# Placing the high and low weight blocks of one gated product at unequal 64-byte shifts

## The reference

```python
def swiglu(x, w_gate, w_up, w_down):
    return (jax.nn.silu(x @ w_gate) * (x @ w_up)) @ w_down

meta = jnp.broadcast_to(meta_tokens[None].astype(x.dtype), (B, N_META, D_MODEL))
h = jnp.concatenate([meta, x], axis=1)                       # 272 rows
h = h + 0.5 * swiglu(rmsnorm_2(h, ffn1_norm), ffn1_w_gate, ffn1_w_up, ffn1_w_down)
```

## Time and profile before

| | |
|---|---|
| median of 3 runs | 912.51 us |
| the runs | 918.71, 912.08, 912.51 us |
| the profiled execution's own time | 918.25 us |
| its span | 916.5 us |
| PE, PEld | 904.2 us (99%), 887.5 us (97%) |
| DVE, ACT | 642.7 us (70%), 525.4 us (57%) |
| granted clock of TensorE, mean | 0.997 |
| sw1 in the span | 355.66 to 486.86 us |

### The profile page before, as it was taken

How to read it: one execution, slowest core, us unless ns; L and a number is a source line. 1 busy time by engine, 2 the same in 40 slices (tenths; PEclk the granted TensorE clock), 3 DMA queues, 4 the chain that set the end, 5 groups by cost and what they waited for, 6 DMA issues and landing times.

```text
span 916.5 us, 18478 instructions
## 1 busy us (share of the span) xinstructions
PE 904.2 (99%) x7425; PEld 887.5 (97%) x7425; DVE 642.7 (70%) x1108; ACT 525.4 (57%) x869; POOL 4.7 (1%) x11
## 2 busy tenths in 40 slices
PE   9999999999999999999999999999999999999996
PEld 8988998999999999999999999999999999999996
DVE  6999888776446765676666547768769877767553
ACT  6897877666336655544444535445675665454452
POOL 1000000000000000000000000000000000000000
PEclk9999999999999999999999999999999999999998
DMA  9751444365765565555556465554415655665641
GB/s 312 248 171 72 139 139 161 93 206 187 234 185 179 175 192 183 171 176 171 179 185 202 149 184 161 161 171 130 162 50 203 186 185 187 198 201 198 208 138 46
DMA packets 110612, 157.63 MB, mean 172 GB/s; under 512 B 9916, under 2 KB 61248, under 8 KB 110400
## 3 DMA queue, kind: packets, MB, share of 16 engines
q1 hardware_dynamic: 109776, 155.19, 53.4%
q10 hardware_dynamic: 576, 0.73, 0.2%
q0 software_dynamic: 176, 0.53, 0.1%
HBM read 155.37 MB, written 1.05 MB: 171 GB/s over the span
## 4 chain that ended last, share of the span: by engine, by line
PE 95%; DVE 3%; ACT 1%; issue 1%; DVEq 0%; ACTq 0%
PE ps L1046 29%; PE ps L1048 29%; PE ps L1047 29%; PE ps L1093 1%; PE ps L1129 1%; PE ps L1060 1%; DVE wl L1819 1%; PE ps L1303 0%; PE ps L1323 0%; PE ps L1261 0%; PE ps L1283 0%; PE ps L1139 0%; ACT wh L1385 0%; DVE S L2070 0%; PE ps L1152 0%
## 5 line engine op out<-in xcount | busy, mean ns | idle before, releaser
L1819 DVE TENSOR_TENSOR wl<-raw,wh 128x1024 fp32r<-128x1024 f32 (+2 forms) x291 | 346.8, 1212 | 197.4 <-ACT wh L1385 196.8
L1385 ACT ACTIVATE wh<-raw 128x1024 fp32r<-128x1024 f32 (+2 forms) x291 | 298.1, 1046 | 193.4 <-PE ps L1048 193.0
L1046 PE MATMUL ps<-U,wh 128*128 128x256 f32 (+2 forms) x1392 | 398.3, 286 | 0.1
L1048 PE MATMUL ps<-U,wl 128*128 128x256 f32 (+2 forms) x1392 | 391.4, 281 | 0.0
L1047 PE MATMUL ps<-UL,wh 128*128 128x256 f32 (+2 forms) x1392 | 390.8, 281 | 0.0
L1046 PEld LDWEIGHTS ps<-U,wh 128*128 128x128 f32 (+1 forms) x1392 | 261.6, 188 | 3.1 <-issue 1.4
L1047 PEld LDWEIGHTS ps<-UL,wh 128*128 128x128 f32 (+1 forms) x1392 | 261.9, 188 | 1.7 <-issue 1.0
L1048 PEld LDWEIGHTS ps<-U,wl 128*128 128x128 f32 (+1 forms) x1392 | 262.3, 188 | 0.0
L1046 PE MATMUL ps<-H,wh 128*128 128x256 f32 (+1 forms) x736 | 208.7, 284 | 0.1
L1048 PE MATMUL ps<-H,wl 128*128 128x256 f32 (+1 forms) x736 | 206.6, 281 | 0.0
L1047 PE MATMUL ps<-HLO,wh 128*128 128x256 f32 (+1 forms) x736 | 206.4, 280 | 0.0
(11 more groups left out here) (340 smaller groups left out, 788.5 us busy)
## 6 DMA issues: line engine op xcount, KB each, us to landing
raw<-w_ff SPq DMA_DIRECT2D x64, 512.0 KB, 4.4
raw<-ffn_w_gate SPq DMA_DIRECT2D x88, 256.0 KB, 3.7
raw<-ffn_w_up SPq DMA_DIRECT2D x88, 256.0 KB, 4.6
raw<-ffn_w_down SPq DMA_DIRECT2D x44, 512.0 KB, 4.6
raw<-w_in SPq DMA_DIRECT2D x40, 512.0 KB, 3.7
raw<-w_out SPq DMA_DIRECT2D x16, 512.0 KB, 3.9
raw<-wkv_x SPq DMA_DIRECT2D x8, 512.0 KB, 3.9
raw<-w_in SPq DMA_DIRECT2D x9, 256.0 KB, 3.1
```

What stands on the lines that cost most here:

```text
L1046: e.matmul(out, sh, xh, start=(i == 0 and n == 0), stop=False)
L1048: mm = e.matmul(out, sl, xh, start=False, stop=(over and n == nk - 1))
L1385: e.activation(wh, raw, ACT.Copy).then_inc(*up("w_hi", v))
L1819: lo = e.tensor_tensor(wl, raw, wh.bitcast(F32), ALU.subtract)
```

## The change

`first_columns` gets one more argument, 0 for the high blocks and 1 for the low ones. For sw1 alone it adds a number of columns from a table of eleven pairs, one pair per group. A column is 4 bytes, so 16, 32 and 48 are 64, 128 and 192 bytes. `tile` and `unit_parts` pass the argument, so PE, ACT and DVE agree on the places. All else is as it was.

```diff
+APART = ((0, 32), (32, 0), (0, 16), (16, 0), (0, 48), (48, 0), (16, 48), (48, 16), (32, 48), (16, 32), (32, 16))
+
+
-def first_columns(name, g, i):
+def first_columns(name, g, i, low):
...
-    return at
+    return [c + APART[g][low] for c in at] if name == "sw1" else at
...
-def split_blocks(parts, half, name, g, i):
-    at, width = first_columns(name, g, i), GEMM[name].width(g)
+def split_blocks(parts, half, name, g, i, low=0):
+    at, width = first_columns(name, g, i, low), GEMM[name].width(g)
...
-        wh, wl = split_blocks(t["wh"], h, name, g, i), split_blocks(t["wl"], low_half(h), name, g, i)
+        wh, wl = split_blocks(t["wh"], h, name, g, i), split_blocks(t["wl"], low_half(h), name, g, i, 1)
...
-    return raw, split_blocks(t["wh"], half, name, g, i), split_blocks(t["wl"], low_half(half), name, g, i)
+    return raw, split_blocks(t["wh"], half, name, g, i), split_blocks(t["wl"], low_half(half), name, g, i, 1)
```

## The result

| | before | after |
|---|---|---|
| median of 16 runs each | 912.1 us | 917.54 us |
| ratio, 95% interval | | 1.0047 [1.0027, 1.0066] |
| the shorter kind | 12 runs, 911.70 to 912.51 | 8 runs, 913.56 to 914.60 |
| the longer kind | 4 runs, 918.53 to 918.80 | 7 runs, 920.47 to 921.08 |
| the profiled execution, its span | 918.25, 916.5 us | 920.47, 918.6 us |

One execution of 4483 us stands outside both kinds; nothing here explains it. With eight executions in the shorter kind and eight above it, the median of 16 is the mean of 914.60 and 920.47 and falls between the kinds; the median of the other 15 would be 914.60. Within a kind the change costs 1.9 us (medians 911.98 and 913.90) and 2.1 us (918.71 and 920.76). The rest of the 5.4 us between the medians comes from the mixture alone. In both kinds the change makes less than 1% of difference.

What follows compares the result with a forecast made beforehand. PE's matmul steps were taken to bound the kernel. Adding 2.0 us for sw1's groups 1 to 10 and 0.1 us for group 0 to a short run's 912.51 us gave 914.6 us, range 911.2 to 921.3.

Steps and rivals of the forecast that it cites:

- The bound: Whole kernel: PE busy 904.2 of 916.5 us, so its length is the number of matmuls times the step between starts.
- The size: sw1: groups 1 to 10 go from 123.7 to 125.8 ns a step; with group 0, +2.1 us in all.
- the steps of uq, gq and small over their floor: 256-column products at other distances: 118.3 and 120 ns against 113.3, giving 125.0 and 126.7 at 272 columns; middle 125.8.
- The splits at nothing, dn1 unchanged: DVE and ACT splits in sw1 cost nothing more (1053 and 1224 ns); dn1 only starts 2.1 us later.
- Distance between load and stream: sw1, groups 1 to 10: weights load 64 bytes ahead of the stream in all three matmuls; other distances lengthen the step.
- Two changes of distance in three loads: Every changed sw1 group: 1 to 3 of three loads leave distance 64, and the distance changes twice in three loads.
- groups 0, 2 and 4: sw1 groups with unshifted high blocks: expected nearer 11.9 us than groups 5 to 10, most groups at 11.9 to 12.3.
- The median: Whole kernel: a short run's 912.51 us plus 2.1 gives 914.6 us as the median; chance 0.43.
- the chance of the longer kind: Whole kernel: the median falls among long executions, at 920.4 us (919 to 923), by the same mechanism; chance 0.25.
- (b): sw1: addresses do nothing, every group stays at 11.87 us, total 912.5 us; chance 0.12.
- (c): sw1: faster, since some shifts reach the 120.0 ns floor (group of 11.52 us); total 908.6 to 912 us; chance 0.15.
- (d): sw1: every load pays 10 ns, 133.7 ns a step, +10.6 us, total 923.1 us; chance 0.05.

Runs made afterwards that it cites:

- e6: Changed kernel plus one unit of ff1a (group 1, unit 0) shifted by 192 bytes; ten executions at 919.93 to 921.04 us, one far outside (1997.95).
- e5: Kernel before the change, with one unit of ff1a (group 1, unit 0) shifted by 192 bytes; eleven executions at 918.00 to 918.78 us.
- e1: Changed kernel, but sw1's groups take equal high and low shifts (0 to 192 bytes) and sw2 the eleven unequal pairs; one execution, 923.96 us.
- e7: Changed kernel, but sw1's groups take finer equal shifts of high and low blocks (0 to 240 bytes); repeated 80-byte shift gave 123.6 and 124.3 ns a step.
- e4: Changed kernel, but all sw1 weight blocks shifted by 128 bytes and both U and UL moved by 128 bytes; sw1's groups 1 to 10 at 11.87 us.
- e3: Changed kernel, but only sw1's low blocks shifted, by 128 bytes in all groups, and UL moved by 128 bytes too; 927.25 us.
- e10: Changed kernel with sw1 back in place, one ff1a unit's high blocks shifted by 128 bytes; seven at 911.43 to 912.70 us, three at 918.17 to 919.00, ratio 1.0011.
- e11: Kernel before the change, rstd sum of ff1a after 11 tiles instead of 12; seven executions at 911.75 to 912.29 us, two at 918.2, one far outside.
- e9: Changed kernel with sw1 back in place, one ff1a unit's high blocks shifted by 128 and low by 64 bytes; nine at 917.90 to 918.56 us, ratio 1.0058.

## Why the prediction was right, point by point

- **The bound.** Right. All of the 2.1 us is in PE's steps in sw1; the granted clock and the splits' times are as they were, and PE still waits for nothing there.
- **The size.** 125.8 ns forecast for groups 1 to 10, 125.8 measured; +2.1 us forecast, +2.11 in the profiles, 1.9 and 2.1 within the kinds, 2.2 in e6 against e5. The rows that carried it were the steps of uq, gq and small over their floor, brought over to 272 columns. That the hit is so close is luck. Single distances cost from nothing to 3.0 ns (e1, e7), and the ten pairs of groups 1 to 10 happen to average 2.1. And the price itself may be another's: uq and gq run at 118.3, next to the pace of 117.8 that e4 shows at the old distance as well as at the new one, and at 272 columns no such second pace was seen.
- **The splits at nothing, dn1 unchanged.** Right, 1224 and 1052 ns; dn1 has 65.35 / 528 = 123.8 ns a step, as before (the 65.1 us forecast for it was low for the kernel before too). One reading behind it was wrong: in groups 1 to 10 the two blocks of a unit lie 512 columns apart, end to end as in sw2; only group 0 has 528. So the earlier trace rows compared splits at other starts, not at another spacing. Nothing in the sum hangs on it.
- **Distance between load and stream.** Right (e4 against e1), but the step behind it failed in its detail: "in all three matmuls" the load was taken to run beside the one stream before its own matmul. e3 gives 124.9 ns where this asks for 123.7, so it is not the whole; what takes its place (both streams, or the distance between the streams too) stays open. It did no harm to the sum, since the price was taken from whole tiles of uq and gq.
- **Two changes of distance in three loads.** Not needed: equal shifts cost the same as unequal ones. And the guess that groups 0, 2 and 4, with the high blocks in place, would be nearest 11.9 was wrong; 12.05 and 12.13 for 4 and 2, and the cheapest is group 5, (192,0), at 11.96.
- **The median.** Here the forecast of 914.6 is 2.9 us low. The step is the chance of the longer kind: I gave its median 0.25, and 7 of 15 executions were long. That a median could fall between the kinds, as it did with the one execution far outside, I had not thought of. Without that one the forecast would have hit, and that too would have been luck: eight executions of one kind against seven of the other. Since the kernel before had 4 of 16, 13 of 20 and 4 of 24 in three comparisons, the share moves by itself, and nothing here shows that the change moved it. The value of either kind was right: 914.6 and 920.4 forecast, 913.9 and 920.8 measured. The mechanism given for them was right too: two paces of the same stream, from 183 to 355 us.
- **Rivals.** (b), no effect, is refuted by e4 against e1. The Trainium skill (SBUF — State Buffer, "Who interferes with whom") has PE's weight load and moving operand on separate ports, with PE never waiting on anyone; here the same blocks at the same places modulo 256 bytes cost 123.7 or 126.4 ns a step by where the stream lies (e4 against group 2 of e1), so the measurement decides against the rule. (c), gains: none of the sixteen equal shifts and none of the change's pairs goes below 123.6. (d) did not occur; no group of the change passed 126.5.

No version beat the kernel before; e10 and e11 equal it within their intervals.

## What to carry to other kernels

Where PE is full and its weights are loaded anew for each matmul, read the step between starts, not the duration, and look at it product by product: 3 ns in 124 is invisible in a busy share and is 2 us here. Place weights and stream at a fixed distance modulo 256 bytes and map that distance by experiment, for each width of the stream, groups of one product taking one value each; one run then gives ten values. At 256 columns, where a pace is held from one product to the next, such a map can mislead: sw2's groups in e1 do not separate the two. Before comparing two kernels by a median, look whether the executions fall into kinds, and compare kind with kind: the change costs 2 us, the medians said 5.4, and 2.9 of these hang on one execution far outside.

## What the runs showed that I had not expected

- Sixteen bytes are enough: an equal shift of 16 costs 2.8 ns a step, one of 32 costs 0.4, one of 80 nothing. A grid of 64 bytes, as the change has it, misses this.
- A 256-column stream with the same distances can hold 113.3 or 117.8 ns a step for 170 us. A wait of 0.47 us is followed by either (the kernel before, e10); a unit of 24 loads at another distance is followed by 117.8 in the profiles of e5, e6 and e9 and, by their times, in all 20 executions of e5 and e9 and in 10 of e6 (its eleventh is far outside). A product can hand its pace on: dn2, with its distances as before, ran at 117.8 behind a slow sw2 (e3). It need not: in e4, ff1b ran at 117.8 and ff2b behind it at 113.3.
- At 272 columns no such second pace was seen: e4's and e10's ten groups, entered at 113.3 ns a step, are at 11.87 us like those of the kernel before, entered at 117.8.
